# Retention in a streaming encoder block: the 16-row tile with its high and low parts in one stationary block

## The reference

```python
proj = h @ w_in                                   # q, k: 4 heads x 256; v, g: 4 heads x 512
q, k, v, g = jnp.split(proj, ...)
q = rope(q); k = rope(k) * QK ** -0.5
s = einsum('bhqd,bhkd->bhqk', q, k) * decay       # by head, causal
o = einsum('bhqk,bhkv->bhqv', s, v) (+ the state of earlier chunks)
on = (o - mean(o)) * rsqrt(var(o) + eps)          # over the 512 values of a head
y = silu(g) * on
return y @ w_out
```

## Time and profile before

| what | value |
|---|---|
| median of three runs | 1374.65 us (1372.19 to 1377.16) |
| the profiled execution's own time | 1370.72 us |
| its span, first to last instruction | 1368.7 us |
| mean granted clock of TensorE | 0.917 of full speed |
| retention, first product to the end of the output product | 25.9 to 537.7 us |
| TensorE / VectorE / ScalarE / GpSimd busy | 1166.4 / 474.0 / 244.9 / 239.1 us |

### The profile page before, as it was taken

How to read it: one execution, slowest core, us unless ns; L and a number is a source line. 1 busy time by engine, 2 the same in 40 slices (tenths; PEclk the granted TensorE clock), 3 DMA queues, 4 the chain that set the end, 5 groups by cost and what they waited for, 6 DMA issues and landing times.

```text
span 1368.7 us, 15208 instructions
## 1 busy us (share of the span) xinstructions
PE 1166.4 (85%) x5784; PEld 725.9 (53%) x5784; DVE 474.0 (35%) x847; ACT 244.9 (18%) x453; POOL 239.1 (17%) x168
## 2 busy tenths in 40 slices
PE   4899999999998998489999927877887748999990
PEld 4889889789696776433333313343443343333330
DVE  5301432332258203512222246264554462222224
ACT  4122132132142112000111110021321400101111
POOL 4233233143044221020000044000000002000004
PEclk8999999999999999589999957979999869999995
DMA  6131141041140124649999346300011084999935
GB/s 250 62 139 62 47 154 62 31 169 62 46 154 1 62 82 201 256 142 306 354 346 339 89 154 238 123 0 1 1 67 56 1 338 157 320 355 359 321 86 215
DMA packets 38673, 212.30 MB, mean 155 GB/s; under 512 B 5376, under 2 KB 5504, under 8 KB 29648
## 3 DMA queue, kind: packets, MB, share of 16 engines
q1 hardware_dynamic: 21168, 151.26, 29.8%
q10 hardware_dynamic: 12704, 43.13, 10.2%
q0 software_dynamic: 4736, 17.04, 3.4%
HBM read 307.75 MB, written 35.78 MB: 251 GB/s over the span
## 4 chain that ended last, share of the span: by engine, by line
PE 66%; issue 12%; DVE 12%; POOL 5%; DMA 3%; ACT 2%; ACTq 0%; POOLq 0%; DVEq 0%
PE ps L744 20%; PE ps L913 16%; PE ps L932 8%; PE ps L968 4%; PE ps L1054 4%; POOL ring_r L1838 4%; PE ps L959 3%; PE ps L901 2%; PE ps L877 2%; PE ps L830 2%; DVE xT L1303 1%; DVE arena L1765 1%; DVE arena L1768 1%; PE ps L890 1%; DMA xT<-slot_rows 1%
## 5 line engine op out<-in xcount | busy, mean ns | idle before, releaser
L913 PE MATMUL ps<-ring,xT 128*64 128x512 f32 x640 | 226.9, 598 | 5.9 <-DVE xT L1303 5.9
L744 PE MATMUL ps<-x_hi,ring_r 128*128 128x264 f32 x1024 | 191.3, 287 | 7.0 <-DVE xT_r L1291 7.0
L1838 POOL TENSOR_TENSOR ring_r<-ring,ring_r 128x1024 fp32r<-128x1024 f32 x56 | 134.1, 2408 | 301.9 <-ACT ring_r L1081 301.9
L913 PE MATMUL ps<-arena,xT 128*64 128x512 f32 x384 | 168.7, 592 | 0.0
L744 PE MATMUL ps<-ring_r,x_hi 128*128 128x512 f32 (+1 forms) x480 | 156.2, 407 | 11.6 <-POOL ring_r L1838 11.6
L744 PEld LDWEIGHTS ps<-x_hi,ring_r 128*128 128x128 f32 x1024 | 160.6, 190 | 7.5 <-DVE xT_r L1291 7.3
L1303 DVE TENSOR_TENSOR xT<-ps,gains 128x512 f32<-128x512 f32 (+1 forms) x100 | 62.0, 665 | 249.6 <-PE ps L901 247.3
L744 PE MATMUL ps<-xT_r,ring_r 128*128 128x264 f32 x512 | 146.3, 286 | 0.0
L932 PE MATMUL ps<-arena 128*64 128x512 f32 x512 | 118.6, 606 | 6.1 <-ACT arena L1204 6.1
L913 PEld LDWEIGHTS ps<-ring,xT 128*64 128x64 f32 x640 | 72.9, 138 | 95.4 <-issue 92.0
L744 PEld LDWEIGHTS ps<-ring_r,x_hi 128*128 128x128 f32 (+1 forms) x480 | 84.6, 177 | 43.2 <-POOL ring_r L1838 13.1
(11 more groups left out here) (225 smaller groups left out, 1481.9 us busy)
## 6 DMA issues: line engine op xcount, KB each, us to landing
ring<-in_w_gu SPq DMA_DIRECT2D x46, 2048.0 KB
arena<-in_w_down SPq DMA_DIRECT2D x74, 1024.0 KB
arena<-in_w_gu SPq DMA_DIRECT2D x28, 2048.0 KB
ring<-in_w_ret SPq DMA_DIRECT2D x48, 512.0 KB, 3.6
slot_out<-arena ACTq DMA_DIRECT2D x64, 256.0 KB, 7.1
xT<-slot_rows ACTq DMA_DIRECT2D x60, 256.0 KB, 5.1
slot_rows<-arena ACTq DMA_DIRECT2D x8, 1024.0 KB, 4.1
ring<-in_w_ret_out SPq DMA_DIRECT2D x16, 512.0 KB, 4.5
```

The costliest lines, as they stand in the source:

```text
L744: last = mm(dst, a_parts[x], b_parts[y], start=(start and n == 0), stop=(stop and n == 2))
L913: last = mm(ps[cols, b, :], xgT[:, k % 2, c, cols], by_row(gu(j))[:, c, :], start=(c == 0), stop=(c == KT - 1))
L1838: G.tensor_tensor(w_lo[slot][:, m], w_raw[slot][:, m], w_hi[to][:, m], ALU.subtract).then_inc(lo_made, 1)
```

## The change

The 16-row tile's high and low activations are laid side by side as the columns of one stationary block, so that one record multiplies both with the high weights and one both with the low weights: two records per step where there were three (the product low x low is now in it too). The result lies in two groups of rows of a PSUM bank, which have to be summed.

For V4 the block is 32 columns of high parts (positions 496 to 527) and 32 of low parts; the copy to `v_tm` takes all 64 rows. The scores of the last 16 positions are computed twice, to output rows 0 to 31 and 32 to 63, and multiplied with a table that is zero for the 16 positions that belong to the tile before; the output product then contracts over 64 rows and so sums the halves. For META in the output product the block is 32 columns of high and 16 of low parts, and VectorE adds two groups of rows to the residual, one after the other. VectorE makes the blocks with small copies: two after the input norm, two in each `split_y`.

```diff
-NCONST = C_IOTA + 128
+C_DECAY = C_IOTA + 128
+NCONST = C_DECAY + HEADS * N_META
...
+        after_arena = sb("after_arena", [128, ARENA - 22048])
+        short_r = sb("short_r", [128, 2 * KT * (SHORT + N_META)], R)
+        x_short = short_r[:, 0:2 * KT * SHORT].rearrange("p (k c) -> p k c", k=KT)
+        y_short = short_r.rearrange("p (k c) -> p k c", k=2 * KT)
...
-            return min(128, POS - 128 * t)
+            return 2 * SHORT if t == NT else 128
...
+            def short_product(dst, both, b_parts, start, stop):
+
+                for n, part in enumerate(b_parts):
+                    last = mm(dst, both, part, start=(start and n == 0), stop=(stop and n == 1))
+                return last
...
+                if z == "a":
+                    pe.wait_ge(short_made, 2)
...
+                            weights = w_hi[0][:, :, k, :], w_lo[1][:, :, k, :]
+                            if t == NT:
+                                last = short_product(columns(b + g, 2 * SHORT), x_short[:, k, :], weights,
+                                                     k == 0, k == KT - 1)
...
-                        for k in range(2):
-                            last = mm(ps[0:key_rows(t), b + g, 0:POS - 128 * t],
-                                      kT[:, k, 128 * t:128 * t + key_rows(t)],
-                                      qT[:, k, 128 * t:POS], start=(k == 0), stop=(k == 1))
+                        for at in ((0, SHORT) if t == NT else (0,)):
+                            for k in range(2):
+                                last = mm(ps[at:at + (SHORT if t == NT else 128), b + g, 0:POS - 128 * t],
+                                          kT[:, k, POS - SHORT:POS] if t == NT else kT[:, k, 128 * t:128 * t + 128],
+                                          qT[:, k, 128 * t:POS], start=(k == 0), stop=(k == 1))
...
+                                if t == META:
+                                    last = short_product(columns(b + g, SHORT + N_META), y_short[:, KT * c + k, :], weights, *ends)
...
+            dve.wait_ge(x_lo_made, 5)
+            V_.tensor_copy(x_short[:, :, 0:SHORT], x_hi[:, :, POS - SHORT:POS]).then_inc(short_made, 1)
+            V_.tensor_copy(x_short[:, :, SHORT:2 * SHORT], x_lo[:, :, POS - SHORT:POS]).then_inc(short_made, 1)
...
-                        last = V_.tensor_tensor(scores_of(t)[0:r], ps[0:r, b + g, 0:n], dec[0:r, 0:n], ALU.mult)
+                        last = V_.tensor_tensor(scores_of(t)[0:r], ps[0:r, b + g, 0:n],
+                                                dec_short[0:r] if t == NT else dec[0:r, 0:n], ALU.mult)
...
                 V_.tensor_copy(hi, yT[:, k, :]).then_inc(y_hi_made, 1)
                 dve.wait_ge(y_hi_made, hd + 1)
-                V_.tensor_tensor(y_lo[:, k, :], yT[:, k, :], hi, ALU.subtract).then_inc(y_split, 1)
+                step.done(V_.tensor_copy(y_short[:, k, 0:SHORT], hi[:, :, 0:SHORT]))
+                step(V_.tensor_tensor(y_lo[:, k, :], yT[:, k, :], hi, ALU.subtract))
+                V_.tensor_copy(y_short[:, k, SHORT:SHORT + N_META], y_lo[:, k, 0:N_META]).then_inc(y_split, 1)
...
-                V_.tensor_tensor(hh, ps[0:N_META, b, :], hh, ALU.add).then_inc(free[b], 1)
+                step(V_.tensor_tensor(hh, ps[0:N_META, b, :], hh, ALU.add))
+                V_.tensor_tensor(hh, ps[SHORT:SHORT + N_META, b, :], hh, ALU.add).then_inc(free[b], 1)
```

More of the change, by code:

```diff
@@ L27 @@
 HEADS, QK, VD = 4, 256, 512
+SHORT = 2 * N_META
 KV_HEADS, HD = 4, 64
@@ L102, in tables @@
         r[:, 2 * POS + h * POS:2 * POS + (h + 1) * POS] = dec
+        for half in range(2):
+            c[SHORT * half + N_META:SHORT * half + SHORT, C_DECAY + h * N_META:C_DECAY + (h + 1) * N_META] = \
+                dec[0:N_META, 0:N_META]
     s = np.zeros((128, NST), f)
@@ L357, in build @@
             "w_hi_made", "w_lo_made", "x_hi_made", "x_lo_made", "y_hi_made", "y_split"))
+        short_made = sem("short_tile_made")
         o_summed, sq_summed = sem("outputs_summed"), sem("squares_summed")
@@ L784, in head @@
                     for g, t in enumerate(tiles):
-                        c = slice(128 * t, 128 * t + key_rows(t))
+                        c = slice(128 * t, 128 * t + 128)
                         for k in range(KT):
-                            last = split_product(columns(b + g, key_rows(t)), (x_hi[:, k, c], x_lo[:, k, c]),
-                                                 (w_hi[0][:, :, k, :], w_lo[1][:, :, k, :]), k == 0, k == KT - 1)
+                            weights = w_hi[0][:, :, k, :], w_lo[1][:, :, k, :]
+                            if t == NT:
+                                last = short_product(columns(b + g, 2 * SHORT), x_short[:, k, :], weights,
+                                                     k == 0, k == KT - 1)
+                            else:
+                                last = split_product(columns(b + g, 128), (x_hi[:, k, c], x_lo[:, k, c]), weights,
+                                                     k == 0, k == KT - 1)
                     last.then_inc(full[b], 1)
@@ L855, in _ @@
                             for k in range(KT):
[L856 to L859, removed]
+                                weights = w_hi[n % 2][:, :, k, :], w_lo[1 - n % 2][:, :, k, :]
+                                ends = c == 0 and k == 0, c == 1 and k == KT - 1
+                                if t == META:
+                                    last = short_product(columns(b + g, SHORT + N_META), y_short[:, KT * c + k, :], weights, *ends)
+                                else:
+                                    last = split_product(columns(b + g, rows(t)),
+                                                         (y_hi[c][:, k, at], y_lo[:, KT * c + k, at]), weights, *ends)
                         if c == 1:
@@ L1382, in head @@
                 dec = decay[:, bass.ds(hd, 1), :].rearrange("p a c -> p (a c)") if z == "r" else decay[:, hd, :]
+                short = con[:, C_DECAY:C_DECAY + HEADS * N_META].rearrange("p (a c) -> p a c", a=HEADS)
+                dec_short = short[:, bass.ds(hd, 1), :].rearrange("p a c -> p (a c)") if z == "r" else short[:, hd, :]
                 b = fl.bank("S0" + z)
```

## The result

| | before | after |
|---|---|---|
| median of five runs, us | 1373.23 | 1366.12 (1364.89 to 1366.66) |
| ratio, 95% interval | | 0.9941 (0.9925 to 0.9957) |
| the profiled execution, us | 1370.72 | 1366.66 |
| TensorE busy, us | 1166.4 | 1155.5 |

A forecast was written before the change was run, and what follows sets the result against it. Retention was taken to be bound by TensorE's queue. The terms -7.41 + 1.15 - 5.56 + 2.9 + 1.7 + 0.6 + 0.2 sum to -6.4 us, so 1374.65 becomes 1368.2 us; range 1363 to 1372 us.

The forecast's parts named there:

- 1 V4, four heads: V4 product: 16 records a head instead of 24, at 0.2317 us each, saving 7.41 us over four heads.
- 2 S34: Scores: the 16-column product done twice adds 4 records a head, costing 1.15 us over four heads; bounds 0 and 3.6.
- 3 output product, three tiles: META tile of the output product: three of four halves lie ahead of other products and save 5.56 us.
- 4 turn in split_y(2): New VectorE copies let one more GpSimd instruction in ahead of the subtraction, delaying VARt: +2.9 us, ends 0.3 and 5.
- 4 clock behind VARt: After some 3.3 us of TensorE idle before VARt, some records run at 1.2 instead of 2.4 GHz: +1.7 us.
- 5 end of retention: W1_4's second half: TensorE's 1.85 us saving counts 0; META's second add costs +0.6 us, bounds 0.5 and 0.8.
- 6 start: Start: the table grows from 348 to 380 KB, with GpSimd's first instruction behind it; +0.2 us, bounds 0 and 0.6.
- Rival D: Loads of the wider stationary blocks are not hidden: slower, 1381 us with 100 ns more a record; chance 0.04.
- Rival B: No turn is lost in split_y(2): part 4 is 0.6 us without clock cost, -10.4 us, 1364.2 us; chance 0.3.
- an idle of 3 to 3.5 us before VARt: Sign in the profile after that TensorE waits for the delayed split_y(2) chain; near 1 us would mean no lost turn.
- What was to stay hidden: split_y(3)'s low copy, +0.5 us, hidden by 1.2 us; splits 0 and 1 need some 0.9 of VectorE's 1.91 us wait.
- Rival C: Clock falls for long: W0_23 and W0_4 at half clock cost 7.3 us, not 1.7; -0.8 us, 1373.9 us; chance 0.1.

The follow-up runs named there:

- experiment 1: Changed kernel with V4, S34 and the score table as before, so only META's output product has two records a step; ratio to before 0.9993.
- experiment 5: The changed kernel run again unedited for a second profile (also called the repeated run); ratio to the kernel before 0.9939.
- experiment 6: Changed kernel with split_y's high copy moved behind the subtraction, next to the low copy; ratio to the kernel before 0.9944.
- experiment 7: Changed kernel with each head's two 16-column score products done four times over, 24 more records a head; ratio to the kernel before 0.9969.
- experiment 3: Changed kernel with head 2's two small copies made later, behind the sum of squares; ratio to the kernel before 0.9934.
- experiment 8: Changed kernel, copies in place, with GpSimd starting the second output chunk's low parts only after split_y(2)'s subtraction; ratio to the kernel before 0.9910.

## Why the prediction was right

The forecast, -6.4 us with TensorE's queue as the bound and one lost turn, held: 7.1 us at the medians, 8.1 and 8.4 by the two ratios. By its steps:

| step | told, us | found, us |
|---|---|---|
| 1 V4, four heads | -7.41 | 4 x (5.56 - 3.68) = -7.5 |
| 2 S34 | +1.15 | 4 x (2.99 - 2.94) = +0.2 |
| 3 output product, three tiles | -5.56 | 3 x (5.56 - 3.69) = -5.6 |
| 4 turn in split_y(2) | +2.9 | +2.55 |
| 4 clock behind VARt | +1.7 | 0 in the first profile after, +1.6 in experiments 1, 5, 6, 7 |
| 5 end of retention | +0.6 | +0.70 |
| 6 start | +0.2 | none seen: the table took 5.88 us, 5.91 in experiment 5, against 6.35 |
| sum | -6.4 | -9.6 or -8.0 |

**Steps 1 and 3** held with their mechanism: a record costs 0.23 us whether its stationary block has 16, 48, 64 or 128 columns. Rival D is out: the loads did get longer, 120 to 135 ns for 93 to 98, and stayed hidden though all of them contract over 128 rows. The Trainium skill (TensorE: Matmul & The Clock Gate, The mechanism) lists that a load overlaps running products only where the row groups differ; this trace does not bear that out. The same section also lets a load go ahead into the background weight buffer, which the prediction left out and with which the trace agrees. The prediction's estimate of 40 and 27 ns more a load, which goes by the page's time per column (section LDWEIGHTS (loading the stationary operand)), holds for the loads' own lengths: 134 and 122 ns on average for 95.

**Step 2 was mis-sized**: I gave S34's small records everything that the big ones' rate by column left over, 0.29 us. Four more of them added 0.05 us (the chain of work has 2.94 us for the 16 records before, 2.99 for the 20 after), so the leftover was not theirs. Experiment 7, 16 ns a record, says the same. The term is 0.95 us too high.

**Step 4** was right down to its rows: a copy of over 2 us, the subtraction above 4 us behind it, GpSimd's fourth part ahead. Rival B is out: with the copy moved (experiment 3) or GpSimd silent (experiment 8) the 2.55 us are gone. Only the sign that I had chosen misled: an idle of 3 to 3.5 us before VARt, or near 1 for B. The changed kernel had 1.8 and 2.4 us, between the two, because the low clock of W0_01 eats into it. The right reading is the distance from MUt, told as 14.3 + 2.9 = 17.2 us and found as 16.85. What was to stay hidden did: the splits 0 and 1 leave 1.31 of VectorE's 1.91 us before the sum of outputs, and split_y(3) ends at 446.84 us, 1.3 us before TensorE asks. The rule of the Trainium skill on single-source copies and the shared ports (SBUF — State Buffer, Who interferes with whom) agrees with the trace: copies of 64 (split_y(0), 2.23 us) and 128 elements (2.29 us) are caught as the cast of 2112 is.

**The clock term** came or did not come. Behind waits of 0.7 and 1.8 us, VARt and W0_23 took 12.1 us; behind 2.4, 2.5, 3.0 and 3.0 us they took 13.7. That is no fixed price of a wait: behind 2.68 us in each of heads 2 to 4, V01 took 12.8, 12.8 and 11.2 us before and 11.2, 14.0 and 12.8 us after. What decides it was not tested. Rival C is out: the low clock lasted for a part of the stretch only, a granted clock of 0.88 over 13.7 us.

**Step 5** held: the last 1.85 us of TensorE's saving bought nothing, and the second add is on the path.

**Where the sum and the profiles part.** From MUt to the router's product the first profile after is 2.34 us shorter than before (123.05 to 120.71), and steps 3, 4 and 5 without a clock term give 5.6 - 2.55 - 0.70 = 2.35; the repeated run is 0.77 us shorter, and with its 1.6 us of clock the steps give 0.75. The difference lies ahead of MUt. There steps 1 and 2 give 7.3 us and the two profiles have 6.45 and 6.54. It is clock: V01 took 50.6 us over the four heads before and 51.8 in the first profile after; in the repeated run it took 50.8, but from the first product to V01 it was 29.7 for 29.1 us. The prediction had no term for this. So a part of the hit is luck: the 0.95 us too much in step 2 about covers these 0.8 us.

Two slips of the prediction changed nothing. Its waits of TensorE leave out 18.2 us that lie ahead of the first product (7.0 on L1291 and 11.2 on L1297). And the bounds of its terms, with the lost turn kept, add up to -9.3 and -2.4 us, not to -8 and -3; the measured values lie inside both, and the lower bound of the range came from rival B.

## What to carry to other kernels

Here a record saved on the saturated engine paid its pitch, up to the next place where that engine waits for another: find each such wait and ask what the edit puts ahead of it. The price of a tiny VectorE copy on the path was set by what GpSimd was doing then, 0.2 us or 2.3; move it to where GpSimd is silent, or let GpSimd wait. Read the distance between two events that another engine sets, not the idle in front of the second.

## What the runs showed that I had not expected

Extra float32 products (32 stationary columns, 16 moving) cost 12 to 16 ns a record inside a stream, though each record is some 180 ns long by itself. Holding GpSimd back by one wait, an edit of two lines, was worth about as much as half of the change under study. And the time from the router's product to the end varied from 821.5 to 837.4 us among kernels that are the same there, more than the whole effect under study: what a change in retention does is read up to the router's product.
